# Tabled head norms, two small identity products ahead of the z products, and one small fp32 product at the head of each gate group, in a two-block transformer kernel

## The reference, cut to what matters

```python
q = partial_rope(rms_norm(q.reshape(B, S, N_HEADS, HEAD_DIM), q_g), cos, sin)

def rms_norm(x, g):
    y = xf * lax.rsqrt(jnp.mean(xf * xf, axis=-1, keepdims=True) + NORM_EPS)
    return (y * g.astype(jnp.float32)).astype(x.dtype)

def partial_rope(x, cos, sin):          # rotates the first 16 of 64 dimensions
    x1, x2, rest = x[..., :half], x[..., half:ROT_DIM], x[..., ROT_DIM:]
    return jnp.concatenate([x1 * c - x2 * s, x2 * c + x1 * s, rest], axis=-1)
```

```python
z = jnp.einsum('td,thkd->thk', xc, u_sel)
a = (jax.nn.gelu(z.astype(jnp.float32)) * g).astype(xc.dtype)
return jnp.einsum('thk,thkd->td', a, v_sel)
```

## Time and profile before

| | us |
|---|---|
| median of 3 runs (lowest, highest) | 1320.14 (1313.42, 1321.28) |
| the profiled execution, its own time | 1320.98 |
| its span, first to last record | 1319.7 |
| PE busy in the span | 1260.2 (95%) |
| DVE busy | 1030.1 (78%) |
| ACT busy | 596.0 (45%) |
| POOL busy | 232.4 (18%) |

### The profile page before, as it was taken

How to read it: one execution, slowest core, us unless ns; L and a number is a source line. 1 busy time by engine, 2 the same in 40 slices (tenths; PEclk the granted TensorE clock), 3 DMA queues, 4 the chain that set the end, 5 groups by cost and what they waited for, 6 DMA issues and landing times.

```text
span 1319.7 us, 21921 instructions
## 1 busy us (share of the span) xinstructions
PE 1260.2 (95%) x8287; PEld 1096.1 (83%) x8287; DVE 1030.1 (78%) x2279; ACT 596.0 (45%) x1105; POOL 232.4 (18%) x180
## 2 busy tenths in 40 slices
PE   5988899988998999999999999999999999999997
PEld 5577865676697679999999999999988888888886
DVE  5588897686777788999578888889877777777776
ACT  1434693546342825456554444444443333334332
POOL 0354000460000006788830000000000000000001
PEclk9999999999999999999999999999999999999999
DMA  9877642856678354555544444444566655565652
GB/s 357 296 238 263 242 142 66 307 202 227 236 259 330 113 187 165 182 185 188 176 147 160 145 145 154 151 147 158 173 198 198 195 194 191 192 192 193 194 196 102
DMA packets 92382, 256.82 MB, mean 195 GB/s; under 512 B 9472, under 2 KB 16896, under 8 KB 91904
## 3 DMA queue, kind: packets, MB, share of 16 engines
q1 hardware_dynamic: 59728, 195.91, 44.9%
q10 hardware_dynamic: 32560, 59.66, 12.7%
HBM read 254.47 MB, written 1.06 MB: 194 GB/s over the span
## 4 chain that ended last, share of the span: by engine, by line
PE 72%; DVE 13%; DMA 5%; POOL 4%; ACT 3%; issue 2%; SPq 1%; DVEq 0%; ACTq 0%; POOLq 0%
PE bank L1824 27%; PE bank L1831 26%; PE bank L693 5%; PE bank L2111 4%; PE bank L1195 2%; DVE arena L434 2%; DMA arena<-in_w_in 2%; PE bank L801 2%; POOL head_ms L824 2%; DVE u_lo L685 2%; DMA arena<-in_nsa_w_in 1%; DVE v_lo L685 1%; ACT arena L980 1%; PE bank L928 1%; DVE arena L972 1%
## 5 line engine op out<-in xcount | busy, mean ns | idle before, releaser
L1824 PE MATMUL bank<-h_hi,u_hi 128*128 128x256 f32 x632 | 180.7, 286 | 1.1 <-ACT arena L1949 1.1
L1824 PE MATMUL bank<-h_lo,u_hi 128*128 128x256 f32 x632 | 176.9, 280 | 0.0
L1824 PE MATMUL bank<-h_hi,u_lo 128*128 128x256 f32 x632 | 176.9, 280 | 0.0
L1824 PEld LDWEIGHTS bank<-h_hi,u_hi 128*128 128x128 f32 x632 | 119.6, 189 | 1.3 <-issue 1.3
L1824 PEld LDWEIGHTS bank<-h_lo,u_hi 128*128 128x128 f32 x632 | 119.5, 189 | 0.0
L1824 PEld LDWEIGHTS bank<-h_hi,u_lo 128*128 128x128 f32 x632 | 119.2, 189 | 0.0
L2207 ACT ACTIVATE u_hi<-raw 128x1024 fp32r<-128x1024 f32 x64 | 68.0, 1062 | 104.3 <-PE bank L1831 104.3
L2207 ACT ACTIVATE v_hi<-raw 128x1024 fp32r<-128x1024 f32 x64 | 68.0, 1062 | 101.1 <-PE bank L1831 101.1
L2268 POOL TENSOR_SCALAR raw<-raw 128x1024 f32<-128x1024 f32 x1 | 2.8, 2812 | 624.3 <-DMA raw<-in_final_g 624.3
L1824 PE MATMUL bank<-h_hi,v_hi 128*128 128x256 f32 x392 | 111.5, 285 | 0.0
L1824 PE MATMUL bank<-h_lo,v_hi 128*128 128x256 f32 x392 | 109.7, 280 | 0.0
(11 more groups left out here) (285 smaller groups left out, 3410.8 us busy)
## 6 DMA issues: line engine op xcount, KB each, us to landing
raw<-in_u SPq DMA_DIRECT2D x128, 512.0 KB, 3.5
raw<-in_v SPq DMA_DIRECT2D x128, 512.0 KB, 3.5
arena<-in_ada_t SPq DMA_DIRECT2D x80, 512.0 KB, 5.1
arena<-in_ada_w SPq DMA_DIRECT2D x12, 512.0 KB, 11.8
raw<-in_nsa_w_in ACTq DMA_DIRECT2D x3, 2048.0 KB, 11.7
arena<-in_moba_w_in ACTq DMA_DIRECT2D x3, 2048.0 KB, 13.8
arena<-in_w_in ACTq DMA_DIRECT2D x3, 2048.0 KB, 10.3
arena<-in_w_query ACTq DMA_DIRECT2D x3, 2048.0 KB, 10.7
```

What stands on the lines that cost most here:

```text
L1824: last = pe.matmul(zbank[k].t[:, 0:S], u[:, c, :], h[:, c, :], start=n == 0, stop=n == 3 * DC - 1)
```

## The change

Three edits.

1. **Tables.** A class `Rotary` makes, for each norm's weights and for both token tiles, two tables on GpSimd: `keep` (weights times cosine on the 16 rotated dimensions, weights alone on the other 48, times the scale) and `swap` (the weights of the partner half times the signed sine). `head_norm` becomes: VectorE times the power into the scratch tile, GpSimd scratch with swapped halves times `swap` into a partner tile, VectorE scratch times `keep`, GpSimd the sum of the two on the rotated dimensions. Four tables are made at the head of NSA, 17 instructions; two, for MoBA, in front of NSA's attention, 9 instructions.
2. **Ahead of z.** Two products of the identity with its own first two columns, in front of the loop over the first 40 blocks.
3. **Gate groups.** One such product in front of the four of every group.

```diff
+            G.did(po.tensor_tensor(self.keep[:, :, 0:ROT], w[:, :, 0:ROT], cosd[:, t0:t0 + n, :], ALU.mult))
+            G.did(po.tensor_copy(self.keep[:, :, ROT:HD], w[:, :, ROT:HD]))
+            G.did(po.tensor_tensor(self.swap[:, :, 0:HALF], w[:, :, HALF:ROT], sind[:, t0:t0 + n, 0:HALF], ALU.mult))
+            m = G.did(po.tensor_tensor(self.swap[:, :, HALF:ROT], w[:, :, 0:HALF], sind[:, t0:t0 + n, HALF:ROT], ALU.mult))
+            if self.post != 1.0:
+                G.need(m)
+                m = G.did(po.tensor_scalar(self.all, self.all, self.post, None, ALU.mult))
+            self.made = m
...
-        m_src = V.did(ve.tensor_tensor(d3, s3, hn[0:np_, 0:n].unsqueeze(2).broadcast_to([np_, n, HD]), ALU.mult))
-        V.need(m_src, m_rows)
-        m = V.did(ve.scalar_tensor_tensor(out=d3, in0=d3, scalar=post, in1=g[0:np_, :].unsqueeze(1).broadcast_to([np_, n, HD]),
-                                          op0=ALU.mult, op1=ALU.mult))
...
-        G.did(po.tensor_tensor(t3[:, :, ROT:ROT + HALF], d3[:, :, HALF:ROT], s_lo, ALU.mult))
-        G.did(po.tensor_tensor(t3[:, :, ROT + HALF:2 * ROT], d3[:, :, 0:HALF], s_hi, ALU.mult))
-        m = G.did(po.tensor_tensor(t3[:, :, 0:ROT], d3[:, :, 0:ROT], cc, ALU.mult))
-        G.need(m)
-        return m_src, G.did(po.tensor_tensor(d3[:, :, 0:ROT], t3[:, :, 0:ROT], t3[:, :, ROT:2 * ROT], ALU.add))
+        m_src = V.did(ve.tensor_tensor(t3, s3, hn[0:np_, 0:n].unsqueeze(2).broadcast_to([np_, n, HD]), ALU.mult))
+        G.need(m_src, table.made)
+        m_rot = G.did(po.tensor_tensor(rot, halves, swap, ALU.mult))
+        V.need(m_src, table.made)
+        m = V.did(ve.tensor_tensor(d3, t3, table.keep[0:np_, at, :].unsqueeze(1).broadcast_to([np_, n, HD]), ALU.mult))
+        G.need(m, m_rot)
+        return m_src, G.did(po.tensor_tensor(d3[:, :, 0:ROT], d3[:, :, 0:ROT],
+                                             partner.rearrange("p (h d) -> p h d", h=n), ALU.add))
...
+        for table in (rot_k[0], rot_q, rot_k[1], rot_kc):
+            table.make()
...
+        G.need(V.last())
+        rot_moba_k.make()
+        rot_moba_q.make()
...
+        T.need(m_ident)
+        for _ in range(2):
+            pe.matmul(banks[0].t[:, 0:2], ident[:], ident[:, 0:2], start=True, stop=True)
...
+        pe.matmul(gate_bank(g).t[:, 0:2], ident[:], ident[:, 0:2], start=True, stop=True)
         for j in range(TOK):
             last = pe.matmul(gate_bank(g).t[:, j * P:(j + 1) * P], one_hot[:, g % 2, j, :].bitcast(F32),
                              weighted[:, g % 2, j, :], start=True, stop=True)
```

More of the change, by code:

```diff
@@ L812, in build, with __init__, make @@
     hn = sb("head_ms", [P, NH])
+    rotary = sb("rotary", [P, 4 * (HD + ROT)])
+    class Rotary:
+        def __init__(self, name, lo, tabs, post, home):
+            self.w, self.tabs, self.post = row(name, lo, lo + HD), tabs, post
+            n = len(tabs)
+            self.all = home
+            self.keep = home[:, 0:n * HD].rearrange("p (t d) -> p t d", t=n)
+            self.swap = home[:, n * HD:n * (HD + ROT)].rearrange("p (t d) -> p t d", t=n)
+        def make(self):
+            n, t0 = len(self.tabs), self.tabs[0]
+            w = self.w.unsqueeze(1).broadcast_to([P, n, HD])
+            G.need(m_rope, m_rows)
+            G.did(po.tensor_tensor(self.keep[:, :, 0:ROT], w[:, :, 0:ROT], cosd[:, t0:t0 + n, :], ALU.mult))
[6 more added lines that the diff above has]
+            self.made = m
     def head_power(src, n, tmp, marks):
@@ L824, in head_power, with head_norm @@
         return G.did(po.tensor_tensor(hn[0:np_, 0:n], hn[0:np_, 0:n], pow_half[0:np_, 0:n], ALU.pow))
-    def head_norm(src, dst, n, g, tab, post, tmp, m):
+    def head_norm(src, dst, n, table, tab, tmp, partner, m):
         s3, d3, t3 = (v.rearrange("p (h d) -> p h d", d=HD) for v in (src, dst, tmp))
-        np_ = src.shape[0]
+        np_, at = src.shape[0], table.tabs.index(tab)
+        halves = t3[:, :, 0:ROT].rearrange("p h (b k) -> p h b k", b=2)[:, :, ::-1, :]
+        rot = partner.rearrange("p (h b k) -> p h b k", h=n, b=2)
+        swap = table.swap[0:np_, at, :].unsqueeze(1).broadcast_to([np_, n, ROT]).rearrange("p h (b k) -> p h b k", b=2)
         V.need(m)
-        m_src = V.did(ve.tensor_tensor(d3, s3, hn[0:np_, 0:n].unsqueeze(2).broadcast_to([np_, n, HD]), ALU.mult))
-        V.need(m_src, m_rows)
-        m = V.did(ve.scalar_tensor_tensor(out=d3, in0=d3, scalar=post, in1=g[0:np_, :].unsqueeze(1).broadcast_to([np_, n, HD]),
-                                          op0=ALU.mult, op1=ALU.mult))
[L835 to L838, removed]
-        G.did(po.tensor_tensor(t3[:, :, ROT:ROT + HALF], d3[:, :, HALF:ROT], s_lo, ALU.mult))
-        G.did(po.tensor_tensor(t3[:, :, ROT + HALF:2 * ROT], d3[:, :, 0:HALF], s_hi, ALU.mult))
-        m = G.did(po.tensor_tensor(t3[:, :, 0:ROT], d3[:, :, 0:ROT], cc, ALU.mult))
-        G.need(m)
-        return m_src, G.did(po.tensor_tensor(d3[:, :, 0:ROT], t3[:, :, 0:ROT], t3[:, :, ROT:2 * ROT], ALU.add))
+        m_src = V.did(ve.tensor_tensor(t3, s3, hn[0:np_, 0:n].unsqueeze(2).broadcast_to([np_, n, HD]), ALU.mult))
[6 more added lines that the diff above has]
+                                             partner.rearrange("p (h d) -> p h d", h=n), ALU.add))
     TURN_LAG = 10.5
@@ L853, in buf_free, with q_tile_use @@
         return [m, T.last()]
-    def q_tile_use(qT, j, tab_g, bufs, lag=TURN_LAG):
+    def q_tile_use(qT, j, table, bufs, lag=TURN_LAG):
         def use(t, ps, m):
-            qn, tmp = bufs[t]
+            (qn, partner), tmp = bufs[t]
             m_power = head_power(ps, 8, tmp[:], buf_free(t, m))
             def second():
-                m_src, mq = head_norm(ps, qn[:], 8, tab_g, t, HD ** -0.5, tmp[:], m_power)
+                m_src, mq = head_norm(ps, qn[:], 8, table, t, tmp[:], partner, m_power)
                 def turn_over():
@@ L879, in q_tile_use, with kv_tile_use @@
         return use
-    def kv_tile_use(kT, v_sb, g, bufs):
+    def kv_tile_use(kT, v_sb, table, bufs):
         def use(t, ps, m):
@@ L890, in second @@
                 V.need(m_v)
-                m_src, mk = head_norm(ps[:, 0:NKV * HD], kn[:, 0:NKV * HD], NKV, g, t, 1.0, tmp[:, 0:NKV * HD], m_power)
+                m_src, mk = head_norm(ps[:, 0:NKV * HD], kn[:, 0:NKV * HD], NKV, table, t, tmp[:, 0:NKV * HD], dup[:, 0:NKV * ROT], m_power)
                 G.need(mk)
@@ L1330, in build @@
         bufs = [(carve([P, 6 * P], s0), carve([P, 512], s0)) for t in range(NT)]
-        qbufs = [(b[0][:, 0:512], b[1]) for b in bufs]
+        qbufs = [((b[0][:, 0:512], b[0][:, 512:512 + 8 * ROT]), b[1]) for b in bufs]
         zT = carve([P, DC, S], s0)
@@ L1350, in build @@
         mz3 = G.did(po.memset(xpe[:, :, :, NCMP:CROWS], 0.0))
+        both = list(range(NT))
+        homes = [carve([P, n * (HD + ROT)], s0) for n in (NT, NT, NT)]
+        rot_k = [Rotary("nsa_k_norm", (i + 1) * HD, both, 1.0, homes[i]) for i in range(2)]
+        rot_q, rot_kc = Rotary("nsa_q_norm", 0, both, HD ** -0.5, homes[2]), Rotary("nsa_k_norm", 0, [NT], 1.0, rotary[:, 0:HD + ROT])
+        size = NT * (HD + ROT)
+        rot_moba_q = Rotary("moba_q_norm", 0, both, HD ** -0.5, rotary[:, 0:size])
+        rot_moba_k = Rotary("moba_k_norm", 0, both, 1.0, rotary[:, size:2 * size])
+        for table in (rot_k[0], rot_q, rot_k[1], rot_kc):
+            table.make()
         V.need(m_ident)
@@ L1435, in cmp_outputs @@
                 m_power = head_power(b.t[:, 0:HD], 1, kc_t[:], [m])
-                _, mk = head_norm(b.t[:, 0:HD], kc_n[:, 0:HD], 1, row("nsa_k_norm", 0, HD), NT, 1.0, kc_t[:], m_power)
+                _, mk = head_norm(b.t[:, 0:HD], kc_n[:, 0:HD], 1, rot_kc, NT, kc_t[:], kc_n[:, HD:HD + ROT], m_power)
                 b.free = mk
@@ L1455, in kv_use @@
         def kv_use(i):
-            return kv_tile_use(kTs[i], vs[i], row("nsa_k_norm", (i + 1) * HD, (i + 2) * HD), bufs)
+            return kv_tile_use(kTs[i], vs[i], rot_k[i], bufs)
         gate_mark, gtmp_read = {}, [None]
@@ L1493, in build @@
         project(kv0, 0, WT, kv_use(0), q0, (kv1,))
-        project_split(q0, q_tile_use(qT, 0, row("nsa_q_norm"), qbufs), cmp0, (w1_tiles[0],))
+        project_split(q0, q_tile_use(qT, 0, rot_q, qbufs), cmp0, (w1_tiles[0],))
         cmp_inputs(0, cmp0, kv1, (cmp1,))
@@ L1498, in build @@
         cmp_inputs(1, cmp1, q1, (w1_tiles[1], z0))
-        project_split(q1, q_tile_use(qT, 1, row("nsa_q_norm"), qbufs, 30.0), z0, (z1,))
+        project_split(q1, q_tile_use(qT, 1, rot_q, qbufs, 30.0), z0, (z1,))
         cmp_hidden(1)
@@ L1633, in build @@
         split_h(0, V)
-        project(moba_kv, 0, WT, kv_tile_use(kT, v1, row("moba_k_norm"), bufs), moba_q0)
-        project_split(moba_q0, q_tile_use(qT, 0, row("moba_q_norm"), qbufs), moba_q1, (moba_z0, moba_z1))
-        project_split(moba_q1, q_tile_use(qT, 1, row("moba_q_norm"), qbufs), moba_z0, (moba_out0,))
```

(3 more changed lines are left out.)

## The result

| | before | after |
|---|---|---|
| median of 8 runs, us (lowest, highest) | 1320.01 (1313.42, 1321.28) | 1325.34 (1323.33, 1332.64) |
| profiled execution, us (its span) | 1320.98 (1319.7) | 1324.7 (1323.4) |
| ratio of the times | | 1.0054, 95% interval 1.0033 to 1.0074 |

The changed kernel is 0.5% slower. The interval doesn't contain "no change", though the size is under the 1% that the prediction held to be measurable. The time stays inside the predicted range (1307 to 1332), but it moved the other way.

What follows compares the result with a forecast made beforehand. TensorE was taken as the bound, never idle in the gate stretch but waiting in the projections. Small products +14.5, z rate -10.4 and tables -9 gave -4.9 us from 1320.98: 1316 us, own range 1309 to 1322, whole range 1307 to 1332.

Steps and rivals of the forecast that it cites:

- The small products' own cost: Gate groups and ahead of z: each small product costs 0.22 us, unhidden; together +14.5 us.
- The rate between the groups: z blocks between and behind gate groups: all turn quick, -5.5 and -0.4 us; if all between are slow, +2.7.
- The rival of the wheel: z products: first blocks stay slow, between groups one block in three quick or none; 1326.5 or 1329 us; chance 27%.
- The rate of the first blocks: First 1008 z products, behind the pair: they turn quick, 114.5 us instead of 119.0, -4.5 us.
- second rival: z products: only one stretch turns quick, the gates or the first blocks, or half of each; 1321.5 us; chance 15%.
- The 262 cycles: z products: a skill page's one distance for 256 columns, 109 ns; by it product order shifts nothing, the 10.4 us term zero.
- first rival: z products: the rate stays a wheel, so no gain from it; 1326.5 us, 1329 with all blocks slow; chance 27%.
- The tables: Norms in NSA's and MoBA's projections: less GpSimd rotation work shortens TensorE's waits; -9 us, bounds 0 and -18.
- the 13.0 us of waits: NSA and MoBA projections: TensorE's waits for low parts of weights and GpSimd's tiles; half counted as gained, 6.5 us.
- the three drops of the clock: Windows behind three projection waits: granted clock 0.83, some 1.7 us lost each, 5.1 in all; half counted, 2.5.
- The making of the tables: Ahead of the first power: 17 small GpSimd instructions cost nothing, or 1 us if their cover is gone.
- one stretch only turns quick: z products: gates quick and first blocks slow, or half of each, since a wait's end decides anew; 1321.5 us; chance 15%.

Runs made afterwards that it cites:

- e7: e4 with each gate group cut in two, the second half behind the fifth product of the next z block; 1313.67 us, ratio 0.9959.
- e8: e4 with each gate group cut in two, the second half behind the second product of the next z block; 1311.58 us, ratio 0.9951.
- e9: e4 with each gate group cut in two, the second half behind the third product of the next z block; 1315.36 us, ratio 0.9977.
- e10: The kernel of e4 unchanged, run for a second profile; 1316.55 us.
- e3: The kernel before with only the small product at the head of each gate group; 1328.99 us, ratio 1.0090.
- e1: The kernel before with only the tables, no small products; 1311.92 us, ratio 0.9963.
- e4: The changed kernel without the small products in the gate groups, so tables and the pair ahead of z; 1312.28 us, ratio 0.9954.
- e13: The kernel before with tables for MoBA's six norms alone, NSA as before, no small products; 1311.26 us, ratio 0.9937.
- e2: The kernel before with only the two small products ahead of the first z blocks; 1318.42 us, ratio 1.0003.
- e14: The changed kernel unchanged, run for a second profile; 1325.35 us.
- e11: e8 without the two small products ahead of the first blocks; 1309.25 us, ratio 0.9930.
- e12: e11 with the first loop turn written out and two small products behind the sixth and eleventh z product of its first block; 1313.76 us, ratio 0.9960.

## Why the prediction was wrong

- **The small products' own cost: right.** 64 x 0.22 = 14.1 us and +0.4 ahead of z were forecast. A group costs 0.224 us more, 14.3 in all. The pair moves the first z product by 0.3, of which 0.1 is left behind the first blocks.
- **The rate between the groups: the step that failed.** "I take the quick one as the likeliest, since five products need not turn the same wheel as four." All quick was to give 5.5 + 0.4 us; it gave 0.5. With five products the pattern of three (slow, slow, quick) became one of two (slow, quick), and the double blocks all fall on its slow side: 48 of 79 blocks were slow, where it was 52 before. The rival of the wheel came nearest, though it expected one block in three quick or none. That the rate is taken on at the hand-over and then kept was right. But a fifth product only gave another pattern with slow blocks in it; what made all long pieces quick, at no cost, was the length of the z pieces between hand-overs (e7 and e8 against e9).
- **The rate of the first blocks: right in size by luck.** 4.5 us were forecast and 4.6 stand in the profile, but the pair doesn't buy them: e10 lost them with the same instructions and e3 had them without. The text had a likely reason under its second rival ("The loop's entry stands behind a wait, whose end decides anew") and gave it 15%.
- **The 262 cycles, and a slip.** The figure that the prediction takes from the Trainium skill, page "TensorE: Matmul & The Clock Gate", section "Back-to-back issue gap", stands there for a product by itself. The trace shows a stream of products, at 113.4 and 117.9 ns, so it neither bears the figure out nor refutes it. And with no gain from the rate the prediction's own sum gives 1326.5 us, the time of its first rival, not of the second as it says.
- **The tables: the second term that was too large.** -9 us was forecast, 5.8 stand in the profile and 5.7 to 7.9 in the medians of e1, e4 and e13. "Of the 13.0 us of waits I take half, 6.5, and of the three drops of the clock half, 2.5" spread the gain evenly. In the profiles it was in MoBA (its first scores start at 300.80 instead of 305.21, -4.4 us; the other 1.4 lie behind them, where the profiles scatter by 8) and none in NSA, where the memory that the prediction named as "late next" has the last word: 117.03 and 117.01. The chain of before had the row (19 us of one transfer, a sixth of the window's 115), and it wasn't read. TensorE's waits for low parts were to be under 3 us together; they are 3.3 + 1.5 + 1.8 = 6.6. An earlier start of that transfer was not tried.
- **The making of the tables costs nothing**, as forecast: GpSimd had been idle for 7.54 us when the first power came.
- **The sum.** Forecast +14.5 - 10.4 - 9 = -4.9. In the profiles 14.3 + 0.3 for the products, -4.6 - 0.5 for the rate and -5.8 for the tables (the 5.5 us and the pair's 0.3) make +3.7, as measured. Without the 4.6 of the first blocks, which no edit is shown to buy, it is some 8; the medians of 8 runs lie 5.3 apart, and which rate the first blocks had in the runs without a profile isn't known. The rival "one stretch only turns quick" had the rate's term nearest (5 us), with 1321.5; the time itself lies nearest to the wheel's 1326.5, where a rate without gain and tables of 9 us make up for each other's miss.

## What to carry to other kernels

Before a gain at a wait is counted, follow the chain to the next transfer that lands at a time of its own: what is won ahead of it, also by a drop of the clock that goes, is waited away in front of it. A filler that is to change how a dense stretch of TensorE runs must be priced as if it brings nothing, since its own cost is sure (0.22 us for a full-precision product of two columns); where a pattern repeats, moving the hand-over adds no instruction and can be tried first. And where a rate is set behind a wait, one profile may show one draw: profile the same kernel several times, on one chip, before an effect of 0.3% is put down to an edit.

## What the runs showed of the hardware

- Products [128 x 128] by [128 x 256] have two steady rates, 113.4 and 117.9 ns, at a granted clock of 1.00, kept over 1008 products and changed only at a hand-over from full-precision products or transposes. In the slow one the distances between starts are 117 to 119 ns and repeat in threes of 353.3 ns; in the quick one they are 113 and 114, 340 ns for three (the changed kernel).
- Between hand-overs of fixed lengths the pattern repeats without a miss over 64 groups: slow, slow, quick with four full-precision products (before, e1, e2, e4, e10, e13); slow, quick with five (the changed kernel, e3, e14); and, with the four cut into two and two around two or five z products, all long pieces quick (e7, e8, e11, e12).
- A product of full precision with two columns in front of four others costs 0.224 us, and one of 128 columns takes the same (0.89 us for four); but two of the 2-column kind by themselves among z products take 0.34 us, and two of 128 columns 0.44 (e12, e7).
- A GpSimd product that starts 0.05 us behind a VectorE product with both inputs in SBUF ends behind it, in all 15 norms of the changed kernel: by 0.18 us with 64 elements per partition (VectorE's takes 0.42), by 0.31 to 0.32 with 128 (0.69).
- A granted clock of 0.83 over 10 us can cost nothing: in e13 two such stretches stand ahead of a weight tile that lands at 116.2 us, and the first scores start at 153.6 us, as with tables and a clock of 1.00 there (153.6 in e1, landing at 116.1).
